# Block attention put between the tiles of its projections by pairs of heads, rotary rotation on VectorE, and modulation sums inside the recurrence's first and last slots

## What is computed

```
def _apply_rope(x, cos, sin):
    x1, x2 = jnp.split(xf, 2, axis=-1)
    ...
    return jnp.concatenate([x1 * c - x2 * s, x1 * s + x2 * c], axis=-1)

def _moba_mixer(h, w_in, q_gain, k_gain, w_out, cos, sin):
    q, k, v = [a.reshape(B, S, H, DH) for a in jnp.split(h @ w_in, 3, axis=-1)]
    q = _apply_rope(_rms_norm(q, q_gain), cos, sin)
    k = _apply_rope(_rms_norm(k, k_gain), cos, sin)
    ...
    p = _masked_softmax(...)      # over the block of 256 keys
    return o @ w_out
```

## Time and profile before

| what | value |
|---|---|
| runs | 2978.41, 2983.67, 2989.41 us; median 2983.67 us |
| the profiled execution | 2980.14 us, span 2978.3 us |
| PE, DVE, ACT busy | 94%, 69%, 55% of the span |
| mean granted PE clock | 0.967 |

### The profile page before, as it was taken

One profiled execution on the slowest core, in us unless ns is written; L12 is line 12 of the kernel. 1 busy time (PEld: TensorE's weight loads), 2 busy tenths in 40 slices (PEclk: granted clock), 3 DMA queues, 4 the chain that ended last, 5 costly groups with the idle time before them and its releaser, 6 DMA issues.

```text
span 2978.3 us, 54309 instructions
## 1 busy us (share of the span) xinstructions
PE 2806.8 (94%) x22735; PEld 2545.3 (85%) x22735; DVE 2062.9 (69%) x2571; ACT 1625.0 (55%) x2317; POOL 159.1 (5%) x164
## 2 busy tenths in 40 slices
PE   5879998999998999899999999999999989999999
PEld 5867777778787999877887889999999879998999
DVE  7768874899995556599998565556555775556554
ACT  2445543688883344378887554446444734445443
POOL 0024430000000021000000000000000000000000
PEclk8989998899998999899999999999999999999999
DMA  8501114599994736189998413544455305543353
GB/s 323 224 2 50 69 62 149 213 355 354 355 355 177 267 141 228 43 305 357 351 358 333 160 43 142 183 170 156 152 180 181 138 30 183 183 155 129 129 183 127
DMA packets 78263, 572.85 MB, mean 192 GB/s; under 512 B 8802, under 2 KB 8802, under 8 KB 9186
## 3 DMA queue, kind: packets, MB, share of 16 engines
q1 hardware_dynamic: 76752, 558.93, 50.7%
q10 hardware_dynamic: 1298, 10.90, 0.9%
HBM read 568.74 MB, written 1.05 MB: 191 GB/s over the span
## 4 chain that ended last, share of the span: by engine, by line
PE 85%; DVE 11%; ACT 2%; issue 1%; DMA 1%; DVEq 0%; SPq 0%; ACTq 0%; PEldq 0%
PE ps L1333 15%; PE ps L1257 12%; PE ps L866 10%; PE ps L868 9%; PE ps L867 9%; PE ps L1354 8%; DVE arena L2158 4%; PE ps L888 1%; PE ps L887 1%; PE ps L889 1%; PE ps L1448 1%; DVE arena L2152 1%; DVE wl L2152 1%; DVE hl L2152 1%; PE ps L990 1%; PE ps L1431 1%
## 5 line engine op out<-in xcount | busy, mean ns | idle before, releaser
L2152 DVE TENSOR_TENSOR wl<-ring,wh 128x1024 fp32r<-128x1024 f32 (+1 forms) x560 | 937.8, 1696 | 462.2 <-ACT wh L1571 456.1
L1571 ACT ACTIVATE wh<-ring 128x1024 fp32r<-128x1024 f32 (+1 forms) x560 | 788.4, 1431 | 509.2 <-PE ps L868 305.4
L866 PE MATMUL ps<-hh,wh 128*128 128x256 f32 x2336 | 678.0, 290 | 48.9 <-DVE hl L2152 40.6
L867 PE MATMUL ps<-hh,wl 128*128 128x256 f32 x2336 | 668.7, 286 | 0.0
L868 PE MATMUL ps<-hl,wh 128*128 128x256 f32 x2336 | 668.4, 286 | 0.0
L866 PEld LDWEIGHTS ps<-hh,wh 128*128 128x128 f32 x2336 | 455.9, 195 | 60.2 <-issue 42.4
L867 PEld LDWEIGHTS ps<-hh,wl 128*128 128x128 f32 x2336 | 456.2, 195 | 2.9 <-issue 2.9
L868 PEld LDWEIGHTS ps<-hl,wh 128*128 128x128 f32 x2336 | 455.8, 195 | 0.0
L1257 PE MATMUL ps<-hidl,wh 128*128 128x256 f32 x1024 | 290.3, 283 | 0.0
L1257 PE MATMUL ps<-hidh,wh 128*128 128x256 f32 x1024 | 290.3, 283 | 0.0
L1257 PE MATMUL ps<-hidh,wl 128*128 128x256 f32 x1024 | 290.3, 283 | 0.0
(11 more groups left out here) (275 smaller groups left out, 4781.0 us busy)
## 6 DMA issues: line engine op xcount, KB each, us to landing
ring<-in_stream SPq DMA_DIRECT2D x532, 1024.0 KB, 4.9
arena<-in_wcmp ACTq DMA_DIRECT2D x2, 2048.0 KB, 10.2
arena<-in_lora ACTq DMA_DIRECT2D x1, 2048.0 KB, 9.8
arena<-in_atm ACTq DMA_DIRECT2D x1, 1762.0 KB, 7.5
x<-in_xT ACTq DMA_DIRECT2D x1, 1024.0 KB
out<-x SPq DMA_DIRECT2D x1, 1024.0 KB, 3.8
arena<-in_rwm ACTq DMA_DIRECT2D x1, 736.0 KB, 12.8
cols<-in_cols ACTq DMA_DIRECT2D x1, 715.0 KB
```

The source lines that it names most:

```text
L866: mm(out, w[0], h[0], start=first, stop=False)
L867: mm(out, w[1], h[0], start=False, stop=False)
L1571: return nc.scalar.activation(out, in_, ACT.Copy)
L2152: return v.tensor_tensor(out, a, b, op)
```

## The change

1. Block attention: the projections run in the order of `SB_TILES`, with their input in `in2`, and S, F and O of each head stand behind them by the new table `MOBA_BEHIND` (`block_attention` on PE; `woven` on ACT and DVE). The stage `att_moba` goes. A head's scores wait for `moba_rotated` of its pair of Q and K tiles.
2. NSA and block attention: the rotation is no matmul. DVE multiplies each half of the partitions of the scaled tile by plus or minus sin, writes it to the other half of `Rb`, and adds.
3. `ada1` is summed in slot -1, `ada23` in pieces of 8, 8 and 16 in slots C and C+1. The preparation of rwo's first blocks and of its input (`prep`, `split_pair`) is spread over slots C and C+1 on ACT and DVE, and the last `ada_blocks` of slot C stands earlier.
4. In `mix`, DVE makes the mixed inputs 4 and 5 earlier (`mixed(4)` behind weight block (2, 2), `mixed(5)` behind `parted(3)`).

```diff
+MOBA_BEHIND = {3: "S0", 4: "S1 F0", 5: "S2 F1", 6: "S3", 7: "O0 F2 S4", 8: "O1 F3 S5", 10: "O2 F4 S6 O3 F5 S7", 11: "O4 F6 O5 F7 O6 O7"}
...
-    parts += [up(g["moba_w_in_2"][0]), up(g["moba_w_out_2"][0])] + mlp(3)
+    parts += [up(g["moba_w_in_2"][0])[SB_TILES], up(g["moba_w_out_2"][0])] + mlp(3)
...
-    at["sin"] = np.concatenate([np.sin(ang)] * 2)
+    at["sin"] = np.concatenate([np.sin(ang), -np.sin(ang)])
...
-    for j in range(n + 2):
+    for j in range(n + 1):
         if j < n:
             steps.append(("linear", j))
         if j - 1 in tiles:
             steps.append(("sum", tiles.index(j - 1)))
         if name == "nsa" and j == n:
             steps += [("gate", 0), ("compress", 0)]
-        if j - 2 in tiles:
-            steps.append(("turn", tiles.index(j - 2)))
+        if name == "moba":
+            steps += [("score", u) for what, u in MOBA_BEHIND.get(j, []) if what == "S"]
...
-    MROT[name] = [at["turn", i] for i in range(len(tiles))]
+    SCORE.update({(name, u): LO[name] + k for k, (what, u) in enumerate(steps) if what == "score"})
...
+        ROTATED = {p: 1 + max(i for i, (ch, _) in enumerate(PAIRS["moba"]) if ch // 2 % 4 == p) for p in range(4)}
...
-                    if g == 0:
+            def ada(name, first=0, end=None):
+                t = claim("lo", LO[name]) if first == 0 else tile("lo", LO[name])
+                n16 = BLK // P
+                end = end or n16 * len(ADA_SUMS[name])
+                for o in range(first, end):
+                    g = ADA_SUMS[name][o // n16]
+                    if g == 0 and o == 0:
                         for a in range(2, C - 1):
                             pe.wait_ge(ada_used, a + 1)
                             kept_busy(3)
-                    pe.wait_ge(ada_used, ADA_LAST[g] + 1)
-                    for j in range(BLK // P):
-                        o = n * (BLK // P) + j
-                        last = mm(t[:, o:o + 1], ada_place(ADA_LAST[g])[:, j * P:(j + 1) * P], ones[:, 0:1], start=True, stop=True)
-                last.then_inc(tile_ready["lo"], 1)
+                    if o == first or o % n16 == 0:
+                        pe.wait_ge(ada_used, ADA_LAST[g] + 1)
+                    j = o % n16
+                    last = mm(t[:, o:o + 1], ada_place(ADA_LAST[g])[:, j * P:(j + 1) * P], ones[:, 0:1], start=True, stop=True)
+                if end == n16 * len(ADA_SUMS[name]):
+                    last.then_inc(tile_ready["lo"], 1)
...
-                ada("ada1")
...
+                    if s == -1:
+                        ada("ada1")
...
                     if on_g:
                         gone("y", g)
                         fin(mm(cl("mean", g), blk64, ys, start=True, stop=True))
+                    if s == C + 1:
+                        ada("ada23", 16, 32)
...
+                    if s == C:
+                        ada("ada23", 0, 8)
                     if on_p:
                         solve_r(p, 1)
+                    if s == C:
+                        ada("ada23", 8, 16)
...
-                ada("ada23")
...
-                    elif what == "turn":
-                        pe.wait_ge(ev("qk_norm"), POST0[name] + i + 1)
-                        mm(claim("lo", m), rotm, Ub[:, 0:512], start=True, stop=True).then_inc(tile_ready["lo"], 1)
...
+            def block_attention():
+                scores, flip, outs = attention("moba")
+                lins, tiles = lin_of("moba"), POST_TILES["moba"]
+                tile_of = {j: m for j, q, m, kind in lins}
+                for i, (j, q, m, kind) in enumerate(lins):
+                    linear(q, m, kind, parts_of="moba" if i == 0 else None, at=INPUT["moba"])
+                    if i - 1 in tiles:
+                        n = tiles.index(i - 1)
+                        pe.wait_ge(ev("qk_sq"), POST0["moba"] + n + 1)
+                        mm(claim("lo", MSUM["moba"][n]), ones, Tb[0][:, 0:512], start=True, stop=True).then_inc(tile_ready["lo"], 1)
+                    for what, u in MOBA_BEHIND[i]:
+                        if what == "S":
+                            pe.wait_ge(ev("moba_rotated"), ROTATED[u // 2])
+                            scores(u)
+                        elif what == "F":
+                            flip(u)
+                        else:
+                            pe.wait_ge(free("lo", tile_of[8 + u // 2]), tile_of[8 + u // 2] // 4 + 1)
+                            outs(u)
...
+                    if s == C:
+                        for j in range(2):
+                            ready(act, "rw", RWN["kr1", C - 1])
+                            act.wait_ge(ev("rw_xy"), rw_at(C - 1, RW_LEVELS, 1))
+                            prep(Q0["rwo"] + j)
                     if on_p:
                         act.wait_ge(ev("rw_n2"), p)
                         let(copy(ys, got("y", p)), "y", p)
-                for j in range(2):
-                    prep(Q0["rwo"] + j)
-                split("rwo", rT)
+                    if s == C:
+                        for i in (0, 1):
+                            split_pair("rwo", rT, i)
                 act.wait_ge(ev("rwkv_done"), 1)
+                for i in (2, 3):
+                    split_pair("rwo", rT, i)
                 act.dma_start(atm, d["atm"]).then_inc(at_side, 16)
...
+                if name == "moba":
+                    exps, flips, out = attention("moba")
+                    wait_done(act, LAST_READ["mlp2"])
+                for i, (j, q, m, kind) in enumerate(lin_of(name)):
                     ready(act, "lo", m)
...
+                    if name == "moba":
+                        for what, u in MOBA_BEHIND[i]:
+                            {"S": exps, "F": flips, "O": out}[what](u)
...
                             parted(j + 1)
-                            mixed(j + 2)
+                            mixed(j + 2 if j < 2 else 5)
                         prep(Q0["rkv"] + 4 * j + i + PREP)
                         if (j, i) in ADA_AT_MIX:
                             ada_blocks(1)
+                        if (j, i) == (2, 2):
+                            mixed(4)
                 parted(4)
-                mixed(5)
                 parted(5)
...
-                    if s == -1:
-                        modulation("ada1")
...
                         tt(cx[:, 512:1024], cx[:, 0:512], ea[:, 0:512], ADD).then_inc(ev("rw_cc"), 1)
+                    if s == -1:
+                        modulation("ada1")
...
+                    if s == C:
+                        ada_blocks(1)
+                    if s == C + 1:
+                        prep(Q0["rwo"] + 1)
...
-                        ada_blocks(1)
+                        if s < C:
+                            ada_blocks(1)
...
+                    if s == C:
+                        prep(Q0["rwo"])
+                        dve.sem_inc(src_ready, 2)
+                        ready(dve, "rw", RWN["y", C - 1])
+                        split_pair("rwo", rT, 0)
+                        split_pair("rwo", rT, 1)
...
-                dve.sem_inc(src_ready, 4)
+                dve.sem_inc(src_ready, 2)
                 dve.sem_inc(ev("rwkv_done"), 1)
-                for j in range(2):
-                    prep(Q0["rwo"] + j)
-                split("rwo", rT)
+                split_pair("rwo", rT, 2)
+                split_pair("rwo", rT, 3)
                 modulation("ada23")
...
                 def turned(i):
-                    m, ch = MROT[name][i], PAIRS[name][i][0]
-                    flat, t2 = QK[:, ch:ch + 2, :].rearrange("p c s -> p (c s)"), Rb[:, 0:512]
-                    ready(dve, "lo", m)
-                    K(tt(t2.rearrange("p (c s) -> p c s", c=2), tile("lo", m).rearrange("p (c s) -> p c s", c=2),
-                         amask("sin")[:, None, :].to_broadcast([P, 2, S]), MUL))
-                    dve.sem_inc(free("lo", m), 1)
-                    K(tt(flat, flat, t2, ADD))
-
-                for j in range(n + 2):
-                    if j - 2 in tiles:
-                        turned(tiles.index(j - 2))
+                    ch = PAIRS[name][i][0]
+                    flat = QK[:, ch:ch + 2, :].rearrange("p c s -> p (c s)")
+                    u, r = (a.rearrange("p (c s) -> p c s", c=2) for a in (Ub[:, 0:512], Rb[:, 0:512]))
+                    for src, dst in ((slice(P // 2, P), slice(0, P // 2)), (slice(0, P // 2), slice(P // 2, P))):
+                        last = tt(r[dst], u[src], amask("sin")[src][:, None, :].to_broadcast([P // 2, 2, S]), MUL)
+                    K(last)
+                    K(tt(flat, flat, Rb[:, 0:512], ADD))
+                    if name == "moba":
+                        dve.sem_inc(ev("moba_rotated"), 1)
+
+                if name == "moba":
+                    masked, scaled, low_part = attention("moba")
+                    for j in range(n):
+                        scored = [u for what, u in MOBA_BEHIND[j] if what == "S"]
+                        prep(Q0[name] + j + PREP)
```

(11 more changed lines are left out.)

61 lines of the change are left out of this document (29 added, 32 removed).

## The result

| what | before | changed |
|---|---|---|
| median of six runs | 2978.44 us | 2963.28 us (2953.09 to 2966.03) |
| the profiled execution | 2980.14 us | 2964.74 us, span 2963.0 us |
| mean granted PE clock | 0.967 | 0.967 |

The ratio is 0.9939, 95% interval 0.9926 to 0.9951: 0.6% less time. I had forecast 2962, range 2951 to 2974.

What follows compares the result with a forecast made beforehand. It took PE to bound the kernel (85% of the chain). Savings of 9.1 + 5.6 + 0.9 + 4.0 = 19.6 us gave 2960.5 from the profiled execution or 2964.1 from the median; forecast 2962 us, range 2951 to 2974.

Steps and rivals of the forecast that it cites:

- The two parts that PE was full in: NSA and block attention's projections: turns leave a PE without idle time; seven in NSA 5.6 us, eight in block attention 6.8.
- 34.0 - 12.4 - 7.2 - 5.3 = 9.1: Block attention: old attention stretch and turns gone, less interleaved head pieces, waits for rotated tiles, and the stage's end, in us.
- The gates: Block attention: PE waits for rotated tiles ahead of S0, S2, S4, S6: 1.6, 1.9, 2.1, 1.6, together 7.2 us.
- The last slot: Block attention's end: O6 waits for `low_part` behind weight preparation, then outputs run at half speed; 5.3 us.
- The halves: Rotation on DVE: the 64x512 multiplications on alternate halves do not overlap; 0.69 us, and 0.84 for the second.
- The recurrence's start: Slot -1 and mix: `ada1` sums vanish in PE's idle time; 0.9 us less, from -1.5 to +2.5.
- The recurrence's end: Slot C to rwo's first linear: sums spread into waits, preparations earlier, variance 1.8 us late; 4 us less.
- VectorE the bound in block attention: Rival, chance 0.15: linears 3 to 8 give DVE about 8.0 us beside PE's 7.5; gain 10 us in all, 2973.
- my walk's waits: Block attention: one tile followed from its linear's end to rotation, giving four waits before scores, 7.2 us.
- The recurrence gives nothing: Rival, chance 0.12: sums at half clock before the variance, start later by 1.5; gain 13 us, 2970.
- No waits at the gates: Rival, chance 0.1: in block attention PE is as full as in stick-breaking; gain 27 us, 2956.
- the change is slower: Rival, chance 0.03: 64x512 instructions on DVE cost x above 0.69 us each; at 2.1 us, 15 us slower, 2998.

Runs made afterwards that it cites:

- recurrence_only: The kernel before with only the edits in the recurrence and in mix; median 2979.7 against 2979.49 us, ratio 1.000.
- recurrence_no_mix: The kernel before with the recurrence's edits but not the one in mix; 2978.34 against 2980.42 us, ratio 0.9993.
- outputs_first: Changed kernel, in block attention's last slot the heads' outputs ahead of the weight preparation on ACT and DVE; 2955.91 us, ratio 0.9931.
- mix_undone: Changed kernel with mixed inputs 4 and 5 made where they were before; 2959.18 us, ratio 0.9931.
- sums_behind_gate: Changed kernel with the last 16 `ada23` sums behind the gate of chunk 7, not between its mean and variance; 2964.04 us, ratio 0.9947.
- rotation_first: Changed kernel, in block attention the rotation ahead of the weight preparation in every slot, ACT's roots too; 2958.11 us, ratio 0.9935.
- both_orders: Changed kernel with outputs_first's edit, and the rotation ahead of the weight preparation only in slots 2, 4, 6 and 9; 2954.96 us, ratio 0.9914.
- attention_only: Changed kernel with the edits in mix and in the recurrence undone; 2967.88 us, ratio 0.9964.
- halves_twice: Changed kernel with both multiplications of halves of the partitions made twice, in NSA and block attention; 2981.46 us, ratio 1.0003.

## Why the prediction was right

The direction and the two large terms were right for the reasons given. The size was forecast too large: 19.6 us less, measured 15.2 in the medians and 15.4 in the profiled executions. That the median came out 1.3 us from the forecast is luck, as said below.

**The two parts that PE was full in.** Right: fewer matmuls on a full PE shortened the program by their time. NSA's period is 6.61 us. Six turns at 0.855 us and one at 1.06 less a new wait of 0.56 are 5.6 us, as predicted; the rest of NSA's numbers is clock. recurrence_only and recurrence_no_mix, with NSA's old code, took 91.65 and 91.66 us, before 93.26; with the rotation moved it was 84.4 us in five kernels and 86.1 to 87.7 in the others. The compression alone took 7.17 us in one of the first five (outputs_first), 8.84 in the changed kernel and 9.71 before.

**Block attention.** Predicted 34.0 - 12.4 - 7.2 - 5.3 = 9.1, measured 10.4. The pieces S, O and F take 0.47, 0.65 and 0.33 us by their steps, 11.6 for eight heads. The gates: from the sum's or the piece's start to the scores', less its step, 1.55, 0.65 (F0, with the step of 0.65 that S has in the earlier trace rows; with 0.47 it is 0.83), 1.08, 1.99 and 1.83 us, 7.1 to 7.3 in all against 7.2. The tile was turned at 2674.70, 8.85 us behind its linear's end (2665.85), against 9.1. The last slot is the mis-sized term: 5.3 predicted, 3.7 measured (4.05 from F7 to O6, less its step of 0.33). The two outputs behind the wait took 1.30 us and not 2.6: they ran at 2.4 GHz, where in stick-breaking attention they had not the earlier trace rows. That is a matter of the execution as well: with the same last slot they took 1.30 us in four kernels and 2.55 in three (mix_undone, sums_behind_gate, rotation_first), and in the first two of these the stage is 102.4 us, 9.2 less than before. The clock of the stage is 1.00, before 0.95. My terms as measured would give 11.5, so about 1 us was lost in no term of mine.

**The halves.** I took 0.69 us for the first and 0.84 for the second; the steps are 0.70 and 0.72. Plain overlap, 0.61 (the step of two additions or multiplications of 128x512 with no wait between them in the trace of the kernel before), is not what these show. By the rule that I cited (the Trainium skill, "VectorE: DVE Perf Modes", section "Two Vector instructions with no wait between them") alternate quadrants do not overlap, and the steps of 0.70 agree.

**The recurrence's start.** -0.9 predicted, -0.5 in the changed kernel, -1.0 to -1.4 in recurrence_only, recurrence_no_mix and mix_undone (162.16, 162.45, 162.49 against 163.54). Over all eleven profiled kernels with the sums in slot -1, slot 0 begins at 161.7 to 163.1 us, over the three without at 163.4 to 163.6: 1.2 less in the mean. The sums vanish in slot -1, as said. The edit in mix moved a wait (4.95 and 1.90 us became 3.57 and 3.80) and in the changed kernel ended mix's last linear 1.0 us later, where I had 0.5 earlier; in both_orders, with the same edit, it ended 1.5 us before that.

**The recurrence's end.** Predicted 4.0, measured 3.9, and partly by luck. The steps behind chunk 7's mean were right: variance late 1.8 us, predicted 1.8; from mean to normalised chunk 2.7 us longer, predicted 3.0; from there to PE 1.7 us (481.29 to 482.97), predicted 1.4. Two terms were mis-sized, and the errors cancel. In slot C I had 1.2 us, up to 3 at half clock; mean to mean went from 18.07 to 21.04 us, 3.0, with a clock of 0.76 in that stretch and 0.81 before. I had taken the 2.03 us of the earlier trace rows as a wait that hides sums, but it is DVE that idles there for PE; PE's own waits in slot C were 1.48 and 0.69 us. The other term is rwo: what is left of its first linear takes 4.7 us behind the wait, at clock 1.00, and not the 6.7 that I had (478.3 to 485) with the first 5 us at half speed. Over nine kernels the mean gain of this place is 2.1 us, half the term. In the whole nothing of it is seen in recurrence_only, at most 5 us in recurrence_no_mix, and more between attention_only and mix_undone.

**The step that was not in the sum: the clock elsewhere.** I priced each place as if the rest stayed as it was. The changed kernel lost 2.2 us in the first chunks, 1.4 between rwo and the last experts (ACT's last three preparations of their weights begin at 1616.71 us before and at 1615.94 now, 0.8 earlier where rwo had been 2.1 earlier), and 1.6 between there and NSA's first linear, where the second norm's matmuls (L912, before L916) took 5.38 us and not 3.69. The 19.6 us from profile to profile became 15.4. The median still landed on the forecast by luck: I had raised the forecast by 1.5 us because the three runs shown had a median of 2983.67, and over six runs that of before was 2978.44, below the profiled execution. From there a gain of 19.6 us would have given 2958.8, and 2963.28 was measured.

**The rivals.** "VectorE the bound in block attention" was the nearest to true: not by its price (my walk's waits came out as predicted), but rotation_first shows VectorE full there, and both_orders and halves_twice agree. In the changed kernel itself VectorE still idled up to 0.8 us a slot, for ACT's `wh`. "The recurrence gives nothing" is not decided: it holds with the old attention and not between attention_only and mix_undone. "No waits at the gates" is refuted, and the price of 64x512 was 0.70 us and not 1.7. The formula of "the change is slower" (8x in block attention, 14x - 3.5 in NSA) has a slip, since at 2.1 us for one it gives 8 us slower and not 15. halves_twice, about x = 0.7, shows both of its parts off: 13.9 us in block attention where it has 5.6, and 1.9 of waiting in NSA where it has 6.3.

## What to carry to other kernels

First ask whether the engine that is relieved was full: moving 15 small matmuls off a full PE gave most of the gain, and the large reordering 1.5 to 2.7 us of its stage. When work is moved to a second engine, write down its time per slot beside the first one's: at 8 of 7.5 us, putting the rotation first gave back over half of the waits that it took away. And order the queue of the helping engine by who waits: one weight preparation put behind the last heads' small copies was worth 3.4 us. Before a gain of 2 to 4 us in one place is called a gain, look at the same place in several kernels that leave it alone.

## What the runs showed of the hardware

- One stretch of code that no kernel changed took 77.3 to 82.3 us over fourteen profiled kernels, at a mean granted clock of 0.94 down to 0.86; the recurrence's end, in nine kernels with one order, took 37.2 to 42.1 us. That is more than the 1.2 and 2.1 us by which the recurrence's start and end were shorter in the mean.
- Work put into PE's waits is not free. With all waits behind the gate filled, 16 one-column sums took 6.7 us instead of 3.6 and the clock stayed at 0.67 of full over 21 us, in which the first 8 us of rwo lie; from chunk 7's mean on it took 21.1 us, and 17.1 to 19.2 in the nine kernels with the sums ahead.
- Two multiplications of 64 partitions by 512 columns, on alternate halves, stand 0.70 us apart and last 0.685 us each, as long as ones of 128 partitions (0.69).
- What sets which stretch runs at half clock in a given kernel is open: no run here holds everything fixed but that.
